# First stage of a two-block transformer kernel: the norm's gain row spread by TensorE, the norm in halves, the roots between weight halves; the embedding roots one weight half later

## The reference, cut to what matters

```python
h = rms_norm(x, pre_norm_gain[i])               # x * rsqrt(mean(x*x) + eps) * gain
proj = h @ w_in[i]                              # 1024 x 4096, eight parts of 512 columns
q, k, v, z_a, b_gate, c_gate, u, z_c = jnp.split(proj, N_IN_PARTS, axis=-1)
...                                             # attention, convolution, gates
mixed = jnp.concatenate([attn, conv_out], axis=-1) @ w_out[i]
x = x + rms_norm(mixed, post_norm_gain[i])
e = rms_norm(p[i] @ w_ple_proj[i], ple_norm_gain[i])
x = x + jax.nn.sigmoid(x @ w_ple_gate[i]) * e
```

## Time and profile before

| | us |
|---|---|
| median of the runs | 925.37 |
| lowest and highest run | 924.06, 926.80 |
| the profiled execution, its own time | 926.18 |
| its span, first to last instruction | 924.5 |
| TensorE busy in the span | 884.9 |
| GpSimd busy | 589.5 |
| VectorE busy | 507.5 |
| ScalarE busy | 322.6 |

### The profile page before, as it was taken

One profiled execution on the slowest core, in us unless ns is written; L12 is line 12 of the kernel. 1 busy time (PEld: TensorE's weight loads), 2 busy tenths in 40 slices (PEclk: granted clock), 3 DMA queues, 4 the chain that ended last, 5 costly groups with the idle time before them and its releaser, 6 DMA issues.

```text
span 924.5 us, 11941 instructions
## 1 busy us (share of the span) xinstructions
PE 884.9 (96%) x4256; PEld 735.5 (80%) x4256; DVE 507.5 (55%) x848; ACT 322.6 (35%) x757; POOL 589.5 (64%) x646
## 2 busy tenths in 40 slices
PE   3999999999999999999999999999998999988997
PEld 3788888888887777888888888888877888866786
DVE  4114647965135279766544400444478877778634
ACT  4114333422124267546111111111113446756632
POOL 6566565776789642217977766777777696645352
PEclk9899999999999999999999999999998999999999
DMA  7443312342422457894322232322222222112102
GB/s 211 125 126 92 92 61 76 92 137 70 136 92 69 137 115 170 210 216 133 114 91 90 84 99 92 91 91 91 91 91 70 69 91 70 47 46 80 57 1 92
DMA packets 76218, 92.70 MB, mean 100 GB/s; under 512 B 11520, under 2 KB 54016, under 8 KB 76160
## 3 DMA queue, kind: packets, MB, share of 16 engines
q1 hardware_dynamic: 71808, 83.54, 28.4%
q0 software_dynamic: 4352, 8.39, 5.4%
HBM read 89.82 MB, written 2.10 MB: 99 GB/s over the span
## 4 chain that ended last, share of the span: by engine, by line
PE 80%; DVE 7%; ACT 5%; POOL 5%; issue 2%; DMA 1%; SPq 0%; POOLq 0%; DVEq 0%; ACTq 0%
PE bank L1735 25%; PE bank L1736 24%; PE bank L1737 24%; POOL wlo L709 2%; PE bank L1932 2%; DVE pT L1687 1%; POOL ms L660 1%; ACT junk L786 1%; POOL rstd L663 1%; PE bank L1905 1%; DVE tok L1642 1%; ACT tok L1153 1%; POOL whi L702 1%; DMA resid<-in_x 1%; ACT o L1133 1%
## 5 line engine op out<-in xcount | busy, mean ns | idle before, releaser
L709 POOL TENSOR_TENSOR wlo<-raw,whi 128x512 fp32r<-128x512 f32 x244 | 334.4, 1390 | 0.0
L702 POOL TENSOR_SCALAR whi<-raw 128x512 fp32r<-128x512 f32 x244 | 165.6, 695 | 214.4 <-PE bank L1737 204.7
L1735 PE MATMUL bank<-actB_hi,whi 128*128 128x512 f32 (+1 forms) x416 | 159.4, 383 | 0.0
L1736 PE MATMUL bank<-actB_lo,whi 128*128 128x512 f32 (+1 forms) x416 | 158.6, 381 | 0.0
L1737 PE MATMUL bank<-actB_hi,wlo 128*128 128x512 f32 (+1 forms) x416 | 158.5, 381 | 0.0
L1735 PE MATMUL bank<-whi,actA_hi 128*128 128x512 f32 x368 | 148.0, 402 | 9.9 <-DVE actA_lo L1182 6.4
L1737 PE MATMUL bank<-whi,actA_lo 128*128 128x512 f32 x368 | 145.8, 396 | 0.0
L1736 PE MATMUL bank<-wlo,actA_hi 128*128 128x512 f32 x368 | 145.7, 396 | 0.0
L1735 PEld LDWEIGHTS bank<-whi,actA_hi 128*128 128x128 f32 x368 | 70.5, 192 | 27.6 <-DVE actA_lo L1182 7.8
L1737 PEld LDWEIGHTS bank<-actB_hi,wlo 128*128 128x128 f32 x416 | 78.2, 188 | 15.0
L1735 PEld LDWEIGHTS bank<-actB_hi,whi 128*128 128x128 f32 x416 | 78.3, 188 | 14.5
(11 more groups left out here) (222 smaller groups left out, 1481.0 us busy)
## 6 DMA issues: line engine op xcount, KB each, us to landing
raw<-in_a_w_in SPq DMA_DIRECT2D x44, 512.0 KB, 3.7
raw<-in_w_in SPq DMA_DIRECT2D x32, 512.0 KB, 3.7
raw<-in_a_w_out SPq DMA_DIRECT2D x16, 512.0 KB, 3.3
raw<-in_b_w_in SPq DMA_DIRECT2D x16, 512.0 KB, 3.4
raw<-in_w_out SPq DMA_DIRECT2D x8, 512.0 KB, 3.6
raw<-in_w_ple_gate SPq DMA_DIRECT2D x8, 512.0 KB, 3.4
gain<-in_a_w_in POOLq DMA_DIRECT2D x8, 512.0 KB, 7.2
raw<-in_a_w_in POOLq DMA_DIRECT2D x8, 512.0 KB, 7.8
```

The lines of the kernel that those rows point to most:

```text
L702: pool.tensor_scalar(H, src[:, i * HALF:(i + 1) * HALF], 1.0, 1.0, ALU.mult, ALU.mult).then_inc(w_hi, 1)
L709: ins = pool.tensor_tensor(L, src[:, i * HALF:(i + 1) * HALF], H.bitcast(f32), ALU.subtract)
L1735: M(out_, whi_, xhi_, start=start, stop=False)
L1736: M(out_, whi_, xlo_, start=False, stop=False)
```

## The change

The gain row is loaded once, as one row of 4 KB into partition 0, by a load that ScalarE issues as its first instruction. Two TensorE products (`gn`) of a column of ones with that row spread it to 128 partitions in two banks, and VectorE copies the banks to `gain`. The 512 KB load on SyncE's queue is gone, and all that was behind it moves up one place. Behind the two products TensorE does twelve transposes of the identity (`warm`) whose output nobody reads.

The norm of a tile is made in two instructions of 512 columns, and TensorE waits for each half by itself. ScalarE makes the rounded half of weight half 0, in one instruction between the squares of tile 0 and those of tile 1, and the squares of tiles 2 and 3 come behind the transposed halves of tiles 0 and 1. On GpSimd the root of tile 2 stands between the rounding and the subtraction of weight half 1. On TensorE the second part of unit 0 for tiles 0 and 1 is drawn forward, between the transposes of tiles 2 and 3 and their first parts. The roots of the embedding move behind the second half of the gate's unit 1.

```diff
     o = []
+    o += [("gn", c) for c in range(2)] + [("warm",)]
     for t in range(T):
-        o += [("tr", "x", t, j) for j in range(2)] + [("Th", "v", 0, 0, t)]
-    o += [("T", "v", 0, kh, t) for kh in range(2) for t in range(T)]
+        o += [("tr", "x", t, j) for j in range(2)]
+        o += [("T", "v", 0, 0, t - 2)] if t >= 2 else []
+        o += [("Th", "v", 0, 0, t)]
+    o += [("T", "v", 0, 0, t) for t in (2, 3)]
+    o += [("T", "v", 0, 1, t) for t in range(T)]
...
             x_load(0)
-            sp.dma_start(gain[:, 0], spread(pre_norm_gain[0:1, :], D)).then_inc(gain_in[0], 16)
             load_half(0)
...
-                for i in range(2):
+                for i in range(2 if n else 0):
                     H, _ = halves_of(u, 2 * (n % 2) + i)
...
-            after[0] = [lambda: root("x", 1, D), lambda: root("x", 2, D)]
+            after[0] = [lambda: root("x", 1, D)]
+            after[0.5] = [lambda: root("x", 2, D)]
             after[1] = [lambda: root("x", 3, D)]
...
-            after[at("gate", 1, 0)] = [lambda t=t: root("e", t, D) for t in range(T)]
             after[at("gate", 0, 1)] = [mask_ws]
+            after[at("gate", 1, 1)] = [lambda t=t: root("e", t, D) for t in range(T)]
...
+            act.dma_start(gain[0:1, 1], pre_norm_gain[0:1, :]).then_inc(gain_in[0], 16)
             square_x(0)
+            act.wait_ge(raw_in[0], LANDED[0, 0])
+            A(halves_of(0, 0, 2)[0], raw[:, 0, :], ACT.Copy).then_inc(w_hi, 2)
             square_x(1)
             for t in range(T):
                 for j in range(2):
                     turned("x", t, j)
-                if t == 0:
-                    square_x(2)
-                    square_x(3)
+                if t + 2 < T:
+                    square_x(t + 2)
...
-            dve.wait_ge(gain_in[0], 16)
-            normed("x", "x", 0, 0, "x")
-            for j in range(2):
-                rest("x", 0, j)
-            normed("x", "x", 1, 0, "x")
+            for c in range(2):
+                dve.wait_ge(pe_block, BLOCK["gn", c])
+                V.tensor_copy(gain[:, 0, c * HALF:(c + 1) * HALF], psum[bank_of(("gn", c))][:, :])\
+                    .then_inc(base_step, 1)
+
+            def normed_x(t):
+                dve.wait_ge(rstd_ready["x"], t + 1)
+                if t >= 2:
+                    dve.wait_ge(pe_block, BLOCK["tr", "x", t - 2, 1])
+                for c in range(2):
+                    half = slice(c * HALF, (c + 1) * HALF)
+                    V.scalar_tensor_tensor(tok[:, t % 2, half], resid[:, t, half], rstd[:, NORMS["x"], t:t + 1],
+                                           gain[:, 0, half], ALU.mult, ALU.mult).then_inc(tok_ready["x"], 1)
+
+            dve.wait_ge(base_step, 5)
+            normed_x(0)
+            rest("x", 0, 0)
+            rest("x", 0, 1)
+            normed_x(1)
             for t in range(1, T):
+                rest("x", t, 0)
                 if t + 1 < T:
-                    normed("x", "x", t + 1, 0, "x")
-                for j in range(2):
-                    rest("x", t, j)
+                    normed_x(t + 1)
+                rest("x", t, 1)
...
+                if kind == "gn":
+                    pe.wait_ge(gain_in[0], 16)
+                    return M(bank[:, :], ones[0:1, :], gain[0:1, 1, b[1] * HALF:(b[1] + 1) * HALF], start=True, stop=True)
+                if kind == "warm":
+                    for n in range(12):
+                        ins = nc.tensor.transpose(bank[:, (n % 4) * P:(n % 4 + 1) * P], ident[:, :], ident[:, :])
+                    return ins
```

More of the change, by code:

```diff
@@ L227, in bank_of @@
         return 4 * (b[1] // 2 % 2) + b[1] % 2
-    return {"sc": lambda i, m: 4 + m, "tw": lambda i: 6, "pv": lambda i: 7, "ta": lambda h: 6,
+    return {"gn": lambda c: 6 + c, "warm": lambda: 3, "sc": lambda i, m: 4 + m, "tw": lambda i: 6, "pv": lambda i: 7, "ta": lambda h: 6,
             "ple": lambda t, c: t + 4 * c, "wt": lambda j: 4 + j, "rw": lambda j: 6 + j,
@@ L488, in emptied @@
                 return c7_made, 14 * g + r + {1: 1, 2: 9, 3: 7, 4: 3, 5: 11, 6: 13}[q % 7]
+            if kind == "warm":
+                return pe_block, BLOCK[b]
             a = b[1]
@@ L491, in emptied @@
                 return (pt_lo[1], a + 1) if b[2] else (pt_lo[0], kt0_steps(a))
-            return {"sc": (scored, 2 * a + b[-1] + 1), "tw": (wt_copied, a + 1),
+            return {"gn": (base_step, 4 + a), "sc": (scored, 2 * a + b[-1] + 1), "tw": (wt_copied, a + 1),
                     "pv": (attn_copied, a // 4 + 1), "ta": (attn_out, a + 1),
@@ L1229, in _ @@
             dve.wait_ge(base_step, 3)
-            dve.wait_ge(tok_ready["x"], T)
+            dve.wait_ge(tok_ready["x"], 2 * T)
             for f in range(NH1):
@@ L1814, in ready @@
                     else:
-                        pe.wait_ge(tok_ready[name], t + 1)
+                        pe.wait_ge(tok_ready[name], 2 * t + j + 1 if name == "x" else t + 1)
                         if name == "h" and t >= 2:
                             pe.wait_ge(h_copied, 2 * t - 2)
+                    return
+                if kind == "warm":
                     return
```

## The result

The changed kernel took 914.54 us (median of 4 runs, 913.91 to 915.21); the kernel before, run beside it, 924.72 us (4 runs, 924.06 to 926.80). The ratio is 0.9886, 95% interval 0.9868 to 0.9905: about 10.5 us less by the ratio (8.8 to 12.2), 10.2 between the medians. The forecast was 912.9 us in a range from 910.8 to 917.5. The profiled execution took 915.21 us with a span of 913.5; the one of before had a span of 924.5.

A forecast was written before the change was run, and what follows sets the result against it. TensorE was taken as the bound, busy 884.9 of 924.5 us, so only its idle or slow places counted. First stage 8.7 plus gate 3.8 gave 12.5 us; 925.37 - 12.5 = 912.9 us, range 910.8 to 917.5.

The forecast's parts named there:

- 8.7 + 3.8: Whole kernel: first stage gains 8.7 us (q at 38.3 instead of 47.0), gate 3.8, sum 12.5 us.
- the late clock: First stage, rival: warm transposes don't bring the upper clock, cold until near 18 us; two us more, 915.2; chance 0.15.
- the low end: Range: first stage without any surcharge and loads 0.3 us earlier, 911.2, less some tenths: 910.8.
- The loads: First stage: without the gain load, weight half 0 lands at 5.9 and tile 1 at 7.2; bounds nothing or 2.7 us.
- The gain row: First stage: ScalarE's row load, issued near 0.8 us, lands at 4.2, with 10.5 as the other bound.
- The rival of a late row: First stage: row lands at 10.5 us, 6.3 of the 8.7 us gone, 919.2; half way, 916; chance 0.11.
- the slower one that needed 16.7: First stage, rival: row landing past 16.7 us uses up the whole gain; at 19 us, 927.7; chance 0.02.
- Spread, copies, warm step: First stage: spread 2.6 us, copies 0.65, warm transposes 1.6 to 2.9; real transposes at 9.3, one us later.
- First products and idle time: First stage: first products at 11.4 instead of 12.34, TensorE's idle time 1.9 us in place of 6.4.
- The clock: First stage: upper clock from somewhere in the first groups on; surcharge 1.0 us instead of 6.3, bounds 0 and 3.4.
- GpSimd's next units: First stage's end: unit 1 split near 25, needed at 27.3; q's first unit split at 34.7, 3.6 us early.
- The gate: Gate's unit 1: moving the roots removes the 2.11 us wait and 1.7 us half-rate surcharge behind it, 3.8 us.

The follow-up runs named there:

- e4: Changed kernel with the 512 KB gain load back second on SyncE's queue, without spread, copies or warm transposes; 917.08 us, ratio 0.991.
- e3: Changed kernel with the embedding's roots back ahead of the gate's half, so the first stage's part alone; 916.92 us, ratio 0.9908.
- e6: Changed kernel with TensorE's products in the old order, second part of unit 0 for tiles 0 and 1 not drawn forward; 916.36 us, ratio 0.9904.
- e8: Changed kernel without warm transposes, GpSimd's subtraction of weight half 0 held until both norm halves of tile 0 are done; 915.37 us, ratio 0.9893.
- f1: Changed kernel measured once more, unaltered, as the measure for kernels run beside it; 914.49 us, ratio 0.9884.
- f3: Changed kernel with six real 128 by 128 by 128 products in place of the twelve warm transposes; 914.80 us, ratio 0.9883.
- f4: Changed kernel with VectorE's second gain copy behind the first norm half of tile 0 and not ahead; 914.61 us, ratio 0.9881.
- e5: Changed kernel with the rounding of weight half 0 given back to GpSimd; 914.73 us, ratio 0.9886.
- e7: Changed kernel with twelve real 128 by 128 by 128 products in place of the twelve warm transposes; 915.84 us, ratio 0.9897.
- e1: Changed kernel without the twelve warm transposes; 915.03 us, ratio 0.9886.
- e2: Kernel before with only the embedding's roots moved behind the second half of the gate's unit 1; 920.89 us, ratio 0.9951.

## Why the prediction was right

The mechanism and the sign were right, and the time lay 1.6 us above the forecast. The forecast gain was 12.5 us, 8.7 + 3.8; measured are 10.5 (8.8 to 12.2), or 11.0 between the two spans, of which 7.8 + 4.0 are in the two places and 0.9 were lost later. Two of its numbers don't add up as written: the late clock gives 912.9 + 2 = 914.9 and not 915.2, and the low end 912.9 - 1.0 - 0.3 = 911.6 and not 911.2. Neither decides anything here.

**The loads.** Forecast: weight half 0 at 5.9, tile 1 at 7.2. Measured: by 5.72 and at 7.12. Against e4 that is at least 2.8 and 2.7 us earlier, at the bound of 2.7. e4 shows that this term is needed: with the spread it brings 2.2 to 2.5 us of the gain.

**The gain row.** I took 4.2 us from an issue near 0.8, with 10.5 as the other end. It was there at 2.3 in the profiled execution and at 3.1 to 3.3 in e3, e6, e8, f1 and f3. The rival of a late row is dead, and so is the slower one that needed 16.7.

**Spread, copies, warm step.** The spread took 3.75 us instead of 2.6, which I had worked out from line 1928 at half its clock. VectorE's copies took 0.69 (0.65). The warm transposes took 2.82, the upper end of 1.6 to 2.9. The real ones began at 8.58 instead of 9.3, as the row came earlier. I called this part alone a loss; the runs say a loss too small to be seen, and equally no gain.

**First products and idle time.** Forecast 11.4 and 1.9 us; measured 11.05 and 1.87. The path at tile 0 cost 0.56 (0.9 in the walk) and at tile 1 0.98 (0.9). e6 puts a price on the drawn-forward order, 1.8 us, which the sum had not named apart. That the norm halves take 1.2 us each beside GpSimd was missed. In the first profile the warm transposes and the slow real ones hid it; in e3 and f1 TensorE stood 0.44 and 0.33 us for the second half of tile 0.

**The clock.** Here is the term that was mis-sized. I set the surcharge of the stage at 1.0 us, with the upper clock "from somewhere in the first groups on"; it was 2.7, since the lower clock lasted through tile 0 and into the transposes of tile 1. The rival of the late clock was thus partly true (1.7 of its 2 us). But the runs show more: idle time and surcharge change places. Where the clock rose early, TensorE waited longer for VectorE and ScalarE (f1 2.4 + 0.8, f4 2.8 + 0.9, e5 3.3 + 1.4, e7 2.5 + 0.1), and where it rose late it waited less (e1 2.0 + 3.2, f3 1.4 + 2.9). Together with the start, q begins between 38.5 and 40.1 in the nine traces that keep the changed loads and order (of seven kernels; e8, which delays a subtraction, had 41.58); 38.3 lies below them all. The sum failed by 0.95 us: surcharge +1.7, start -0.7, idle time as forecast. That the error is so small is in part luck, since the start was early only because the row landed at 2.3 in this execution. One stage also differs from one execution to the next, by 0.9 us between before (47.00) and e2 (46.07), which are the same there.

**GpSimd's next units.** Forecast: q's first unit split near 34.7, needed at 38.3. In the profile after it ended at 36.07 and TensorE came at 39.25, so 3.2 us of cover were left of the 3.6.

**The gate.** Forecast 3.8; 4.0 in the pair of traces, 4.5 (3.0 to 6.1) in e2, but 2.4 between e3 and the changed kernel. The 2.1 us of the wait are in both traces that keep the old place of the roots. The 1.7 us of half rate behind it are in one of the two. The new order produced no wait later: the only waits of TensorE between 275 and 330 us after are 0.9 us in two places, for `tok`, and none near 305. The cover behind it was partly thinner than forecast: the roots took 7.3 us, and GpSimd had the gate's unit 2 split at 300.26 and stood until TensorE freed a place at 302.50, so about 2.2 us of cover instead of 3.8. The scaled embedding was ready at 293.2, 4.8 us before its use (forecast 5).

**The base.** I subtracted from 925.37; the kernel before took 924.72 in the runs beside the changed one. The forecast gain was thus 12.5 where 10.2 came out between these medians. 0.9 of the 2.3 us is the stage. I take the rest to be what moves from execution to execution, such as the stretch near 840, whose work ran at the upper clock in the trace of before; no run isolates it.

The record shows one thing more about this base. The 23 runs of the kernel before beside the experiments spread over 4.9 us, and the longer ones have the lower mean granted clock: the six at 0.993 took 922.97 to 923.92, the five at 0.990 or less 926.56 to 927.86. The four runs of e2, which lacks only the gate's wait, lie within 0.8 us, the nine of the changed kernel within 1.7. Against the short ones e2 (920.89) gains 2.1 to 3.0 us, little more than the bare wait. So part of what the change removes seems to be there in some executions only, and the trace of before (926.18) is not one of the short ones. No trace of a short one exists to show it.

## What to carry to other kernels

In a stage where TensorE is short of work, price the start, the waits and the clock as one sum and not each at its best: an earlier clock turns into more waiting, and a filler that is there only to raise it shifts time between the two. Look for a load of which all but a row is redundant ahead of the first data, since it costs all that is behind it. And where the granted clock falls behind a stall, the stall's own length is a sure gain, while the slow stretch behind it may not come in every execution.

## What the runs showed of the hardware that was not expected

- A load of 4 KB from ScalarE's queue, issued at 0.79 us beside the bulk loads of SyncE, was there within 1.5 to 2.5 us, while the small loads behind the bulk in SyncE's queue took 9.7.
- The broadcast of one 4 KB row to 128 partitions by a load took the rate of all transfers from over 400 GB/s to between 191 and 259; with the load gone the fall was gone, and in e4, with the load back, the rate was 218 to 253 again.
- Two float32 products with a single row as input (four records of 512 columns) took 3.75 us. Two with 128 rows had taken 1.32 at the upper clock, so even half the clock leaves 1.1 us that I can't explain.
- VectorE's norm half of 512 columns took 0.70 us alone and 1.2 to 1.6 on average beside GpSimd's subtraction (2.43 for two in the first profile, 2.83 in f1, 3.22 in e3), which itself went from 2.49 to 3.49 us (2.95 in f1 and e3) for 1024 columns.
- The same gap of 2.1 us at the gate was followed by 3.5 us at clock 0.51 in the kernel before and by products at full rate in e3. Near 840 it is the other way round: after a wait of 1.77 us the changed kernel has the stretch at clock 0.66, while the kernel before has the same wait (1.76) and runs on at the upper clock.
